# A hybrid decoder block on one core: both channel-mixer projections by Strassen's seven products, the activations between them in DRAM

## The reference, cut to what matters

```python
h = rms_norm(x, g_pre_mlp[l]) * (1.0 + sc2) + sh2
y = jnp.square(jax.nn.relu(h @ w_fc1[l])) @ w_fc2[l]
x = x + gt2 * rms_norm(y, g_post_mlp[l])
```

## Time and profile before

| what | us |
|---|---|
| median of three runs | 1578.88 |
| lowest, highest run | 1574.45, 1579.76 |
| profiled execution: span from first to last instruction | 1575.3 |
| profiled execution: a time of its own | none is listed |
| start of the first FC1 matmul, end of TensorE's work | about 862.7, 1565.2 |

### The profile page before, as it was taken

How to read it: one execution, slowest core, us unless ns; L and a number is a source line. 1 busy time by engine, 2 the same in 40 slices (tenths; PEclk the granted TensorE clock), 3 DMA queues, 4 the chain that set the end, 5 groups by cost and what they waited for, 6 DMA issues and landing times.

```text
span 1575.3 us, 20573 instructions
## 1 busy us (share of the span) xinstructions
PE 1508.9 (96%) x7590; PEld 1263.8 (80%) x7590; DVE 827.5 (53%) x1445; ACT 565.6 (36%) x1092; POOL 331.8 (21%) x453
## 2 busy tenths in 40 slices
PE   2997998999999999999998999999999999999997
PEld 2886787888888888888877788888888888888886
DVE  6759736678888888854326532323232232323145
ACT  2534434555666566632226412213030302112131
POOL 3315431332322222212114201001010101011012
PEclk9999997899999999999999999999999999999999
DMA  9388772222211211265505220203030211202025
GB/s 353 76 261 250 207 187 82 59 63 66 66 40 53 58 40 38 86 189 154 180 14 187 81 66 28 81 1 106 0 91 15 68 39 40 67 17 90 0 84 183
DMA packets 129073, 148.24 MB, mean 94 GB/s; under 512 B 18405, under 2 KB 98789, under 8 KB 128999
## 3 DMA queue, kind: packets, MB, share of 16 engines
q1 hardware_dynamic: 124266, 132.64, 28.0%
q0 software_dynamic: 4736, 14.68, 2.6%
...
...
## 4 chain that ended last, share of the span: by engine, by line
PE 86%; DVE 6%; ACT 2%; DMA 2%; issue 2%; SPq 1%; POOL 1%; POOLq 0%; DVEq 0%; ACTq 0%
PE ps L1486 24%; PE ps L1488 24%; PE ps L1487 24%; PE ps L1677 4%; PE ps L1693 2%; PE ps L1644 2%; PE ps L1694 2%; PE ps L1645 2%; DVE acc L1218 1%; DVE ada_acc L1095 1%; DVE bk L1160 1%; PE ps L1650 1%; SPq L427 1%; DVE pt_lo L1274 1%; ACT r_swap L804 1%
## 5 line engine op out<-in xcount | busy, mean ns | idle before, releaser
L1486 PE MATMUL ps<-act_hi,a_hi 128*128 128x512 f32 x960 | 392.2, 408 | 1.6 <-DVE a_lo L1074 1.3
L1488 PE MATMUL ps<-act_hi,a_lo 128*128 128x512 f32 x960 | 375.2, 391 | 0.0
L1487 PE MATMUL ps<-act_lo,a_hi 128*128 128x512 f32 x960 | 375.0, 391 | 0.0
L1488 PEld LDWEIGHTS ps<-act_hi,a_lo 128*128 128x128 f32 x960 | 180.6, 188 | 38.5
L1486 PEld LDWEIGHTS ps<-act_hi,a_hi 128*128 128x128 f32 x960 | 181.4, 189 | 34.1 <-issue 1.9
L1053 ACT ACTIVATE relu<-ps 128x512 f32<-128x512 f32 x64 | 38.2, 597 | 468.7 <-PE ps L1488 468.7
L1487 PEld LDWEIGHTS ps<-act_lo,a_hi 128*128 128x128 f32 x960 | 181.5, 189 | 28.4
L1486 PE MATMUL ps<-b_hi,hid_hi 128*128 128x512 f32 x512 | 199.2, 389 | 0.0
L1487 PE MATMUL ps<-b_lo,hid_hi 128*128 128x512 f32 x512 | 199.2, 389 | 0.0
L1488 PE MATMUL ps<-b_hi,hid_lo 128*128 128x512 f32 x512 | 199.2, 389 | 0.0
L720 POOL TENSOR_TENSOR relu<-relu 128x512 f32<-128x512 f32 x64 | 67.3, 1051 | 583.3 <-ACT relu L1053 583.3
...
## 6 DMA issues: line engine op xcount, KB each, us to landing
raw<-in_w_fc SPq DMA_DIRECT2D x64, 512.0 KB, 4.0
ada<-in_w_ada SPq DMA_DIRECT2D x48, 512.0 KB, 5.8
raw<-in_w_in SPq DMA_DIRECT2D x28, 512.0 KB, 4.2
...
mg<-g_dram SPq DMA_DIRECT2D x16, 512.0 KB, 3.9
xt<-in_x SPq DMA_DIRECT2D x8, 512.0 KB, 7.7
q_st<-q_dram SPq DMA_DIRECT2D x8, 512.0 KB, 3.3
raw<-in_w_out SPq DMA_DIRECT2D x8, 512.0 KB, 4.4
```

The source lines that it names most:

```text
L1486: pe.matmul(dst, wh, mh, start=start, stop=False)
L1487: pe.matmul(dst, wh, ml, start=False, stop=False)
L1488: return pe.matmul(dst, wl, mh, start=False, stop=stop)
```

## The change

The matrices of both projections are cut into 2x2 blocks, and the product of two such matrices is made by seven block products of sums and differences of blocks in place of eight block products, in Winograd's form of Strassen's scheme (the intermediate sums u are shared). One level, in two phases.

**Phase 1, FC1.** 8 chunks (512 hidden channels each, in two blocks of 256). The left operands are four blocks of w_fc1 (128x1024 tiles) and four combinations of them, made by GpSimd in five slots that change roles from chunk to chunk (`left_combine`); the right operands are four blocks of the activations, B11, B21, B22 (B12 is used in combinations only), and T1 to T4, made and split once at the head and kept. A product is 2 x 4 x 3 matmuls. Its splits go through a ring of three. Some products are added onto a bank that still holds the one before (`three_more`). ScalarE copies partial sums out (`u_copies`), VectorE adds a bank and a copy to a quarter of the hidden block, squares its ReLU (`quarter`), and SP stores it to `h_dram`.

**Phase 2, FC2.** 4 chunks of 1024 hidden channels. Left operands are blocks of the hidden activations read back from `h_dram`, right ones blocks of w_fc2, each 1 MB (128x2048), four loaded and four combined on each side (GpSimd: `h_combine`, `w2_combine`). A product is 4 x 4 x 3 matmuls; ScalarE and VectorE split both operands anew for each product, through a ring of two. VectorE takes each bank out per token tile (`evacuate`); GpSimd adds shared partial sums to the quarters of y (`add_to_y`, 12 operations of 128x512 a chunk).

**Head and tail.** The second half's transposes come behind the first two products of FC1. At the end, the gate, the norm and the residual are applied for the lower 512 tokens after product 26 of FC2, and for the upper ones with product 27; x1 is read back in 8 loads after the last split. Loops in the mixer are written out.

```diff
--- before.py
+++ after.py
...
+PRODUCTS = 7
+FC1_CHUNKS, FC2_CHUNKS = D_FF // 512, D_FF // 1024
+FC1_RING, FC2_RING = 3, 2
+X_OPS = ("B11", "B21", "T2", "T3", "T1", "T4", "B22")
...
+LEFT_SLOTS = rotated((0, 2, 4, 3, 1), FC1_CHUNKS)
+RIGHT_SLOTS = rotated((4, 2, 0, 1, 3), FC2_CHUNKS)
+LEFT_SOURCE = (0, 1, 0, 2, 4, 3, 1)
+RIGHT_SOURCE = (0, 1, 4, 2, 0, 1, 3)
+LEFT_COMBINED = (None, None, 3, 2, 1, None, 4)
+RIGHT_COMBINED = (None, None, 2, 3, 1, 4, None)
...
+    w1s = [place(f"w1s{i}", kb, [P, 4, 256], f32) for i, kb in enumerate((16, 20, 24, 28, 4))]
+    w1_hi = [place(f"w1_hi{i}", kb, [P, 4, 256], f32r) for i, kb in enumerate((164, 8, 184))]
...
+    hs = [place(f"hs{i}", kb, [P, 4, CH], f32) for i, kb in enumerate((96, 16, 168, 144, 8))]
+    w2s = [place(f"w2s{i}", kb, [P, 4, CH], f32) for i, kb in enumerate((104, 24, 176, 152, 184))]
+    hr_hi = [place(f"hr_hi{i}", kb, [P, 4, CH], f32r) for i, kb in enumerate((32, 48))]
+    hr_lo = [place(f"hr_lo{i}", kb, [P, 4, CH], f32r) for i, kb in enumerate((64, 80))]
+    wr_hi = [place(f"wr_hi{i}", kb, [P, 4, CH], f32r) for i, kb in enumerate((40, 128))]
+    wr_lo = [place(f"wr_lo{i}", kb, [P, 4, CH], f32r) for i, kb in enumerate((72, 136))]
...
+        def load_hidden(j, role):
+            slot = LEFT_SLOTS[j][role]
+            if j:
+                sp.wait_ge(mlp_lo, left_split(PRODUCTS * (j - 1) + 2 + role))
+                if role == 0:
+                    sp.wait_ge(left_comb, 4 * (FC1_CHUNKS + j))
...
+        def load_w2(j, role):
+            slot, k, half = RIGHT_SLOTS[j][role], (0, 1, 0, 1)[role], (0, 0, 1, 1)[role]
+            if j:
+                sp.wait_ge(mlp_lo, right_split(PRODUCTS * (j - 1) + 2 + role))
+                if role == 0:
+                    sp.wait_ge(right_comb, 4 * j)
+            sp.dma_start(w2s[slot][:, :, :], w_fc2_v[j, k, :, :, half * CH:(half + 1) * CH]).then_inc(wide_in[3 + slot], 16)
...
+        def left_combine(at, count, split, base, j, x):
+            a, b, c, d, e = (at[i] for i in LEFT_SLOTS[j])
+            if x == 0:
+                pool.wait_ge(left_in[LEFT_SLOTS[j][2]], count(j, 2))
+                pool.wait_ge(left_in[LEFT_SLOTS[j][3]], count(j, 3))
+                if j:
+                    pool.wait_ge(mlp_lo, split(PRODUCTS * j - 1))
+                out, in0, in1, op = e, c, d, ALU.add
+            elif x == 1:
+                pool.wait_ge(left_in[LEFT_SLOTS[j][0]], count(j, 0))
+                pool.wait_ge(left_comb, base + 4 * j + 1)
+                out, in0, in1, op = c, a, c, ALU.subtract
+            elif x == 2:
+                pool.wait_ge(mlp_lo, split(PRODUCTS * j))
+                pool.wait_ge(left_comb, base + 4 * j + 2)
+                out, in0, in1, op = a, e, a, ALU.subtract
+            else:
+                pool.wait_ge(mlp_lo, split(PRODUCTS * j + 1))
+                pool.wait_ge(left_comb, base + 4 * j + 3)
+                out, in0, in1, op = b, b, a, ALU.subtract
+            pool.tensor_tensor(out[:, :, :], in0[:, :, :], in1[:, :, :], op).then_inc(left_comb, 1)
...
+        def h_combine(j, x):
+            if j == 0 and x == 0:
+                pool.wait_ge(mlp_mm, 2 * ALL_FC1)
+            left_combine(hs, hidden_loads, left_split, 4 * FC1_CHUNKS, j, x)
...
+        w1_combine(0, 2)
+        for k in range(4):
+            pool.wait_ge(t12_made, 2 * k + 1)
+            pool.wait_ge(h2_made, KT + 2 * k + 2)
+            pool.tensor_tensor(h2f[1][:, k, :], h2f[1][:, 4 + k, :], h2f[1][:, k, :], ALU.subtract).then_inc(t34_made, 1)
...
+            pool.tensor_tensor(h2f[0][:, 4 + k, :], h2f[0][:, 4 + k, :], t2f[:, k, :], ALU.subtract).then_inc(t34_made, 1)
+        for j in range(1, FC1_CHUNKS):
+            for x in range(4):
+                w1_combine(j, x)
...
+        h_combine(0, 0)
+        h_combine(0, 1)
+        h_combine(0, 2)
+        w2_combine(0, 2)
+        h_combine(0, 3)
+        w2_combine(0, 3)
+        for j in range(FC2_CHUNKS):
+            for part in range(3):
+                add_to_y(j, part)
+            if j + 1 < FC2_CHUNKS:
+                h_combine(j + 1, 0)
+                h_combine(j + 1, 1)
+                w2_combine(j + 1, 0)
+                h_combine(j + 1, 2)
+                w2_combine(j + 1, 1)
+                w2_combine(j + 1, 2)
+                h_combine(j + 1, 3)
+                w2_combine(j + 1, 3)
...
+                act.activation(u_ab[x % 2][:, m, :], ps[:, 4 * (j % 2) + m, :], ACT.Copy).then_inc(u_copy, 1)
...
+            if n >= FC2_RING:
+                act.wait_ge(mlp_mm, fc2_count(n - FC2_RING, 3))
+            else:
+                act.wait_ge(mlp_mm, (2 * ALL_FC1 - 12, 2 * ALL_FC1 - 4)[n])
+            act.activation(hr_hi[n % 2][:, :, :], hs[slot][:, :, :], ACT.Copy).then_inc(mlp_hi, 1)
...
+        w1_hi_part(2)
+        x_hi_part("T2")
+        u_copies(0)
+        w1_hi_part(3)
+        x_hi_part("T3")
...
+        def t1_t2(k):
+            dve.wait_ge(h2_made, KT + 2 * k + 1)
+            dve.wait_ge(h2_lo, k + 1)
+            dve.tensor_tensor(h2f[0][:, k, :], h2f[1][:, k, :], h2f[0][:, k, :], ALU.subtract).then_inc(t12_made, 1)
+            dve.wait_ge(h2_made, KT + 2 * k + 2)
+            dve.wait_ge(t12_made, 2 * k + 1)
+            dve.tensor_tensor(t2f[:, k, :], h2f[1][:, 4 + k, :], h2f[0][:, k, :], ALU.subtract).then_inc(t12_made, 1)
...
+            for m in range(2):
+                dve.wait_ge(mlp_mm, 2 * n + m + 1)
+                dve.wait_ge(u_copy, u_count(j, made, m))
+                dve.tensor_tensor(c[:, x, m, :], ps[:, bank + m, :], u[:, m, :], ALU.add).then_inc(part_made, 1)
+            dve.wait_ge(part_made, c_count(j, x, 1))
+            dve.scalar_tensor_tensor(out=c[:, x, :, :], in0=c[:, x, :, :], scalar=0.0, in1=c[:, x, :, :], op0=ALU.max,
+                                     op1=ALU.mult).then_inc(c_sq, 1)
...
+        for k in range(4):
+            t1_t2(k)
+            if k:
+                x_lo_part("T2", (k - 1,))
+        x_lo_part("T2", (3,))
+        w1_lo_part(2)
+        w1_lo_part(3)
+        x_lo_part("T3")
+        w1_lo_part(4)
+        x_lo_part("T1")
+        quarter(1)
+        w1_lo_part(5)
+        x_lo_part("T4")
+        w1_lo_part(6)
+        x_lo_part("B22")
+        for n in range(4, ALL_FC1):
+            quarter(n)
...
+            elif n == ALL_FC1 - 3:
+                fc2_left_lo(0)
+                fc2_right_lo(0)
+            elif n == ALL_FC1 - 2:
+                fc2_left_lo(1)
+            elif n == ALL_FC1 - 1:
+                fc2_right_lo(1)
...
+        for n in range(ALL_FC2):
+            j, i = n // PRODUCTS, n % PRODUCTS
+            last = j == FC2_CHUNKS - 1
+            for t in range(4):
+                if i:
+                    evacuate(n, t)
+                if last and i == 6:
+                    final_scale(0, t, 1)
                     if t:
-                        final(t - 1)
-                    if t >= 2:
-                        dve.wait_ge(out_st[t % 2], 16 * (t // 2))
-                    final_scale(t)
-        mlp(0, first=True)
-        with dve.Fori(1, D_FF // CH - 1) as j:
-            mlp(j)
-        mlp(D_FF // CH - 1, last=True)
-        final(TT - 1)
+                        final(4 + t - 1, 12 + t)
+            if n + FC2_RING < ALL_FC2:
+                fc2_left_lo(n + FC2_RING)
+                fc2_right_lo(n + FC2_RING)
+            if last and i == 5:
+                dve.wait_ge(mlp_lo, right_split(ALL_FC2 - 1))
+                dve.wait_ge(gt_in, 32)
+                for t in range(4):
+                    final_scale(1, t, 0)
+                    final_scale(1, t, 1)
+                    final_scale(0, t, 0)
+                for t in range(4):
+                    final(t, 3 * t + 2)
+        final(TT - 1, 16)
...
+        def fc1_product(n):
+            j, i = n // PRODUCTS, n % PRODUCTS
+            hi, lo = w1_hi[n % FC1_RING], w1_lo[n % FC1_RING]
+            x_hi, x_lo = x_op[X_OPS[i]]
+            bank = 4 * (j % 2) + (2 if i in (1, 4, 6) else 0)
+            pe.wait_ge(mlp_lo, n + 1)
+            for m in range(2):
...
+                    if j == 0 and m == 0:
+                        if i < 2:
+                            pe.wait_ge(h2_lo, 4 * i + k + 1)
+                        else:
+                            pe.wait_ge(xt_lo, 4 * (i - 2) + k + 1)
+                    w = slice(m * P, (m + 1) * P)
+                    ops = ps[:, bank + m, :], hi[:, k, w], lo[:, k, w], x_hi[:, k, :], x_lo[:, k, :]
+                    ins = three_more(*ops) if i in (2, 3, 6) else three(*ops, k == 0, k == 3)
+                ins.then_inc(mlp_mm, 1)
...
+        def fc2_product(n):
+            j, i = n // PRODUCTS, n % PRODUCTS
+            bank = 4 * (i in (2, 4, 6))
+            pe.wait_ge(mlp_lo, right_split(n))
+            for t in range(4):
...
+                else:
+                    pe.wait_ge(part_made, e_count(j, i - 3, t))
+                tok = slice(t * P, (t + 1) * P)
```

(41 more changed lines are left out.)

642 lines of the change are left out of this document (420 added, 222 removed).

## The result

The changed kernel takes 1553.33 us (median of 4 runs, 1551.23 to 1554.45) against 1577.88 (4 runs of before, 1574.45 to 1579.76): ratio 0.9844, 95% interval 0.9829 to 0.9859. That is 24.6 us faster, inside the range, 7.3 us over the forecast of 1546. One of the four executions of experiment 8 took 1640.04 us in a slower state, at a granted clock of 0.838, and only its three others are compared.

What follows compares the result with a forecast made beforehand. TensorE, busy 96% of the span, was taken as the bound. 1575.3 - 87.0 + 12 (head) + 3 (clock) + 21.6 (chunk changes) + 9.4 (phase boundary) + 10 (tail) = 1544.3, given as 1546 us, range 1530 to 1560.

Steps and rivals of the forecast that it cites:

- Matmuls, -87.0: Channel mixer: 3072 matmuls become 2688, 384 fewer at 0.2265 us each, -87.0 us; FC1 stays under TensorE.
- Head, +12 and 1.5 for the clock: Start of FC1: third product waits for VectorE until about 891, +12 us; one granted-clock fall here, 1.5 us.
- before's own stall: Kernel before: TensorE loses 6.1 us from the head until 1565.2, set against 18 lost in the changed kernel.
- Chunk changes, +21.6: FC2: GpSimd and VectorE take turns, so products 1', 2', 3' come 1.4, 2.9, 2.9 us late; 7.2 x 3.
- My sum of 84.7 us of turns: FC2 chunk: VectorE low parts 32.2 plus GpSimd work 52.5 must take turns, 84.7 us in 76.1.
- Phase boundary, +9.4 and 1.5: FC1 to FC2: left combinations start only after FC1; product 1 late 1.9, product 2 7.5 us; clock fall 1.5.
- The straight-line prices: FC2 operations of 2048, extended from 512 and 1024: ScalarE 1.90, VectorE 2.30, GpSimd 4.62 us.
- Tail, +10: End of kernel: VectorE's queue behind product 26 puts the end 20 us behind TensorE, before 10.1; +10 us.
- The turns don't reach TensorE: Rival, FC2: both FC2 terms vanish, head +8, one clock fall; 1508 us, chance 0.25.
- GpSimd falls behind: Rival, FC2: two combinations per low part, FC2 terms double; 1575 us, chance 0.12.
- Transfers bind: Rival, FC2: loads one behind another land 27 us late, times three, 81; 1625 us, slower, chance 0.10.
- The pace: Rival, mixer matmuls: pace above 0.2265 us; at 0.240 the 2688 matmuls give back 36 us; chance 0.03.

Runs made afterwards that it cites:

- experiment 8: Changed kernel with the first FC2 chunk's combinations moved from GpSimd to VectorE's queue; 1533.37 us, ratio 0.9729 to the kernel before.
- Experiment 9: Changed kernel with GpSimd's third and fourth head weight combinations later, the tail's y11 and y22 scalings earlier, final operation split; 1550.17 us, ratio 0.9821 to the kernel before.
- run 2: Changed kernel with GpSimd's combinations of FC2's chunks 1 to 3 cut to one column of each 512; 1536.89 us, ratio 0.9744 to the kernel before.
- 3: Changed kernel with each GpSimd combination of FC2's chunks 1 to 3 replaced by three constant fills that read nothing; 1537.3 us, ratio 0.9744 to the kernel before.
- 1: Changed kernel with each GpSimd combination of 2048 elements in FC2 split into two of 1024; 1546.39 us, ratio 0.9807 to the kernel before.
- 4: Changed kernel with GpSimd's 12 additions per chunk cut to one column in FC2's chunks 1 to 3, combinations whole; 1558.61 us, ratio 0.9869 to the kernel before.
- 5: Changed kernel with GpSimd's fifth combination in FC2's chunks 1 to 3 done twice; 1569.37 us, ratio 0.994 to the kernel before.

## Why the prediction was right, and where it was off

**Matmuls, -87.0.** Right: 0.2266 from start to start, FC1 without a wait behind its head.

**Head, +12 and 1.5 for the clock; measured 19.5.** The order of late work was right: the third product waits for VectorE's low part of its weights. I had it at 891, 28.3 us after FC1's first matmul; it came at 894.58, 34.9 us after. That 6.6 us covers the whole excess of 6.0. Mis-sized: I put GpSimd's T3 subtractions into VectorE's way, but not its third and fourth weight combinations, nor the T4 subtractions. The third combination hit the last x1 scale, which has one SBUF input (2.7 us); I had counted two-input operations alone. The fourth and the T4 subtractions stretched two T2 low parts and the weights' low part by 4.3 us together; the T3 turns behind the first low part took 2.2 where I had 2.6. Experiment 9, which moved both combinations, shortened FC1 by 2.7 to 3.9 us against the nine runs with the head as it was. One slip of the sum: the forecast's terms for before's own stall, 691.6 us less 3024 x 0.2265, give 6.7 where it has 6.1; the trace, counted from FC1's first start, gives 6.1.

**Chunk changes, +21.6; measured 18.4.** Right in mechanism, in place (products 1', 2', 3') and nearly in size (late by 1.25, 2.36 and 2.34 us against 1.4, 2.9, 2.9). It was chained out by hand from the turns; the runs show that this is what it is. Without GpSimd's turns it is gone (2, 3), halving their length takes 0.7 us of 6.1 (1), turns outside the stretch don't matter (4), and one turn more costs its own length (5). My sum of 84.7 us of turns in a chunk of 76.1 was the wrong argument for a right result: 14 us of them can go without a gain, and with VectorE at 66 of 76 there is no wait at all. The stretch between the buffer coming free and the first late product is what has to hold.

**Phase boundary, +9.4 and 1.5; measured 21.2.** This is the step that failed in size: product 1, forecast 1.9 us late, was on time, and product 2, forecast 7.5 us late, was 18.6 late. I let the three hidden combinations begin when FC1 ends, and put one weight combination among them. GpSimd's queue has two weight combinations ahead of them, whose second half landed at 1197 only, so the first hidden one began at 1203.13, 13 us after FC1's end at 1189.9. I had named the order of the queue but not the landing of what stands at its front. Part of the 13 us is the hidden half's own: in experiment 8, where VectorE makes the first one, it begins 5.0 us after FC1's end. The straight-line prices held (4.52 to 4.64, 2.28, 1.90).

**Tail, +10; measured 8.3.** Right, and in the right engine; experiment 9 points to VectorE's queue from the last low parts on as its bound; no run tests that by itself.

**The sum.** 1544.3 against a span of 1552.7: head +6.0, boundary +10.3, changes -3.2, tail -1.7, and -3.1 that belongs to the spread. So two terms were 16.3 us too low together, and three smaller errors the other way, one of them chance, bring it to 8.3. The mechanism earned the direction and the place of every loss; that the time stayed 7.3 us from the forecast and inside 1530 to 1560 is in part luck.

**The rivals.** "The turns don't reach TensorE" fell: 25.9 and 3.3 us of waits for low parts. "GpSimd falls behind" fell: the two alternate one by one wherever both are ready. "Transfers bind" fell at the chunk changes (run 2); at the boundary one landing held up GpSimd's queue, and 19.2 of 21.2 us went with its combinations moved (8). The pace is unchanged.
